# Outputs of 32 experts: stored by row of the token with an indirect DMA, instead of by slot and gathered afterwards

## What is computed

```python
u = rmsnorm(h, g_ffn)                         # 512 x 1024
g_idx = argmax(u @ w_group + b_group)         # one of 4 groups
top_v, top_i = top_k(within, 2)               # 2 of the 8 experts in that group
w_sel = softmax(top_v) * p_sel
for e in range(32):                           # D_EXPERT = 256
    hid = silu(u @ w1[e]) * (u @ w3[e])
    y = y + combine[:, e:e + 1] * (hid @ w2[e])
return h + y
```

## Time and profile before

| what | value |
|---|---|
| median of 3 runs | 713.04 us (712.62 to 713.07) |
| the profiled execution's own time | 711.57 us |
| its span | 710.1 us |
| busy PE / DVE / ACT / POOL | 84% / 33% / 29% / 19% of the span |
| share of 16 DMA engines, SP's queue | 45.1% (122.83 MB) |
| the same, ACT's queue (the stores of `yh`) | 3.3% (8.39 MB) |
| the same, POOL's software queue | 3.9% (8.53 MB) |

### The profile page before, as it was taken

One profiled execution on the slowest core, in us unless ns is written; L12 is line 12 of the kernel. 1 busy time (PEld: TensorE's weight loads), 2 busy tenths in 40 slices (PEclk: granted clock), 3 DMA queues, 4 the chain that ended last, 5 costly groups with the idle time before them and its releaser, 6 DMA issues.

```text
span 710.1 us, 9100 instructions
## 1 busy us (share of the span) xinstructions
PE 597.8 (84%) x3367; PEld 383.8 (54%) x3367; DVE 235.1 (33%) x511; ACT 207.2 (29%) x377; POOL 136.1 (19%) x208
## 2 busy tenths in 40 slices
PE   3699999999996988998999689987888788887830
PEld 3598688885663554664555345544444444444510
DVE  5652323233647483454255611111111111111105
ACT  6542314334553533553243311211111111111110
POOL 8200002111247521533100021111111111111022
PEclk9999999999999998999999889989999989999985
DMA  8900000019200010000400569999999999999938
GB/s 249 384 9 1 1 0 1 1 54 329 116 1 0 1 59 1 1 0 13 196 30 30 208 240 377 389 396 398 401 404 397 397 400 397 402 395 397 394 118 308
DMA packets 39056, 140.18 MB, mean 197 GB/s; under 512 B 8480, under 2 KB 10576, under 8 KB 30576
## 3 DMA queue, kind: packets, MB, share of 16 engines
q1 hardware_dynamic: 29680, 122.83, 45.1%
q0 software_dynamic: 4224, 8.53, 3.9%
q10 hardware_dynamic: 5120, 8.39, 3.3%
HBM read 131.28 MB, written 12.65 MB: 203 GB/s over the span
## 4 chain that ended last, share of the span: by engine, by line
PE 61%; DMA 15%; SPq 9%; DVE 7%; issue 4%; ACT 1%; POOL 1%; ACTq 0%; POOLq 0%; DVEq 0%
PE ps L1644 16%; DMA w<-in_w 11%; PE ps L1919 10%; PE ps L1683 7%; PE ps L1774 6%; PE ps L1763 6%; SPq L589 4%; PE ps L1946 3%; SPq L596 3%; PE ps L1827 3%; SPq L590 2%; PE ps L1739 2%; PE ps L1879 1%; DMA yg<-y_rows,pos_y 1%; DMA x<-in_x 1%
## 5 line engine op out<-in xcount | busy, mean ns | idle before, releaser
L1919 PE MATMUL ps<-w,xt 128*64 128x256 f32 x1024 | 134.8, 422 | 42.4 <-issue 32.0
L1919 PEld LDWEIGHTS ps<-w,xt 128*64 128x64 f32 x1024 | 88.3, 152 | 100.0 <-issue 74.9
L1509 DVE TENSOR_TENSOR xt<-ps,g_ffn_c 128x512 f32<-128x512 f32 x32 | 22.1, 691 | 231.3 <-PE ps L1879 231.3
L784 POOL DMA_INDIRECT xg<-u_rows,idx x32 | 29.8, 931 | 284.4 <-PE ps L1879 214.4
L1946 PE MATMUL ps<-w,hT 128*64 128x512 f32 x256 | 61.8, 604 | 0.0
L1068 ACT ACTIVATE hsb<-ps 128x256 f32<-128x256 f32 x32 | 12.3, 383 | 166.0 <-PE ps L1919 166.0
L1683 PE MATMUL ps<-w_oa,mixT 128*128 128x512 f32 x96 | 46.0, 616 | 2.0 <-issue 2.0
L1774 PE MATMUL ps<-probT,vals 128*128 128x512 f32 (+4 forms) x160 | 42.6, 410 | 0.0
L1763 PE MATMUL ps<-qT,kT 68*128 68x400 f32 (+9 forms) x160 | 42.2, 407 | 0.1
L1393 DVE TENSOR_REDUCE nmax<-ps 128x1 f32<-128x528 f32 (+1 forms) x64 | 28.0, 499 | 33.5 <-PE ps L1740 33.5
L719 POOL TENSOR_SCALAR_AFFINE_SELECT probT<-probT 128x128 f32<-128x128 f32 (+2 forms) x80 | 20.2, 271 | 87.7 <-ACT probT L991 87.2
(11 more groups left out here) (277 smaller groups left out, 899.4 us busy)
## 6 DMA issues: line engine op xcount, KB each, us to landing
w<-in_w SPq DMA_DIRECT2D x96, 1024.0 KB, 25.8
y_rows<-yh ACTq DMA_DIRECT2D x64, 128.0 KB, 6.7
w_oa<-in_w_o SPq DMA_DIRECT2D x1, 3072.0 KB, 17.5
x<-in_x SPq DMA_DIRECT2D x4, 512.0 KB, 7.3
w_in_v<-in_w_in SPq DMA_DIRECT2D x1, 2048.0 KB, 11.0
w_in_k<-in_w_in SPq DMA_DIRECT2D x1, 2048.0 KB, 16.0
w_in_q<-in_w_in SPq DMA_DIRECT2D x1, 2048.0 KB, 19.9
u_rows<-u2n SPq DMA_DIRECT2D x4, 512.0 KB, 2.6
```

The lines of the kernel that those rows point to most:

```text
L784: pool.indirect_dma_start(out=xg[e % 2][:, :, :].rearrange("p k n -> p (k n)"), out_offset=None, in_=u2_rows, in_offset=bass.IndirectOffse ...
L1919: ins = pe.matmul(ps[j * slots:(j + 1) * slots, 2 + b, 0:F], xt[b][:, k, :], w13[s][:, j, k, :], start=(k == 0), stop=(k == DK - 1))
```

## The change

The outputs of an expert are scattered at once to their tokens' rows. `y_rows` becomes 512 * 2 rows of 1024: row 2 * token + k for the token's choice k. Seen as half rows of 512 (`y_halves`), the half q of that row is number 4 * token + 2 * k + q, which fits the layout of `yh`.

- `pair_i` (2 * token + k, by POOL's iota) takes the place of `tok`; `pair_f` is 2 * pair - 2048 and is what `tok_hot` is multiplied by. `slot_hot` is 128 wide (the 64 slots twice) and made by two instructions. The index product so gives 128 rows. DVE adds `half_f` (2048 on the first 64 partitions, 2049 on the others) for `idy`, the half-row numbers, and shifts `idy` right by two for `idx`, the tokens. Empty slots are out of bounds in both.
- ACT no longer issues DMAs in the experts' loop. POOL issues one indirect DMA an expert (`scatter_rows`), four experts behind the gather that it follows in POOL's stream. It skips empty slots.
- The eight gathers at the end are gone. SP waits for all scatters and loads four tiles of 1 MB, in which each partition reads the two rows of its token, 8 KB in one piece, into `yg[t]`.
- The overflow branch is written anew to fit (not shown; it isn't taken), and `pos_y`, `late` and the zeroing of `y_over` are gone. The table's initial value is 1024 instead of 0.

```diff
-        yg = [place(f"yg{n}", [P, D], F32, r_qk + 4096 * n) for n in range(2 * NT)]
+        yg = [place(f"yg{t}", [P, 2, D], F32, r_qk + 8192 * t) for t in range(NT)]
...
+        slot_hot = late_new("slot_hot", [P, NT, 2, 2 * slots])
...
-        y_rows = nc.dram_tensor("y_rows", [MAIN + NE * REST, D], F32).ap()
+        y_rows = nc.dram_tensor("y_rows", [SEQ * 2, D], F32).ap()
...
+        y_halves = y_rows.rearrange("r (q d) -> (r q) d", q=2)
+        y_tiles = y_rows.rearrange("(t p k) d -> t p k d", p=P, k=2)
...
+            for b in range(2):
+                sp.wait_ge(y_stored[b], 16 * NE // 2)
+            for t in range(NT):
+                sp.dma_start(yg[t][:, :, :], y_tiles[t]).then_inc(yg_in[t], 16)
...
-            pool.iota(tok[:, :], pattern=[[P, NT]], base=0, channel_multiplier=1).then_inc(masks_made, 1)
+            pool.iota(pair_i[:, :, :], pattern=[[2 * P, NT], [1, 2]], base=0, channel_multiplier=2).then_inc(masks_made, 1)
...
-            step(pool.iota(tok_off[:, :], pattern=[[P, NT]], base=-SEQ, channel_multiplier=1))
-            pool.tensor_copy(tok_f[:, :], tok_off[:, :]).then_inc(masks_made, 1)
+            step(pool.tensor_copy(pair_f[:, :, :], pair_i[:, :, :]))
+            pool.tensor_scalar(pair_f[:, :, :], pair_f[:, :, :], 2.0, float(-2 * 2 * SEQ), ALU.mult, ALU.add
+                               ).then_inc(masks_made, 1)
...
-            step(pool.memset(zero_i[:, :], 0))
+            step(pool.memset(zero_i[:, :], 2 * SEQ))
...
+            def scatter_rows(e):
+                pool.wait_ge(y_copied, e + 1)
+                pool.indirect_dma_start(
+                    out=y_halves, out_offset=bass.IndirectOffsetOnAxis(ap=idy[:, e:e + 1].bitcast(U32), axis=0),
+                    in_=yh[e % 2][:, :], in_offset=None, bounds_check=2 * 2 * SEQ - 1, oob_is_err=False
+                ).then_inc(y_stored[e % 2], 16)
+
+            LAG = 4
             for e in range(NE):
...
+                if e == LAG:
+                    pool.wait_ge(idy_made, 1)
+                if e >= LAG:
+                    scatter_rows(e - LAG)
+            for e in range(NE - LAG, NE):
+                scatter_rows(e)
...
-            def fetch_outputs(source):
-                for b in range(2):
-                    pool.wait_ge(y_stored[b], 32 * NE // 2)
-                for t in range(NT):
-                    for k in range(2):
-                        n = 2 * t + k
-                        pool.indirect_dma_start(
-                            out=yg[n][:, :], out_offset=None, in_=source,
-                            in_offset=bass.IndirectOffsetOnAxis(ap=pos_y[:, t, k:k + 1].bitcast(U32), axis=0)
-                        ).then_inc(yg_in[n], 16)
...
-                    act.wait_ge(y_stored[b], 32 * (RING // 2 * it + s // 2))
+                    act.wait_ge(y_stored[b], 16 * (RING // 2 * it + s // 2))
                 act.activation(yh[b][:, :], ps[:, 6 + b, :], ACT.Copy).then_inc(y_copied, 1)
-                act.wait_ge(y_copied, e + 1)
-                for q in range(2):
-                    act.dma_start(y_main[e, :, q * 512:(q + 1) * 512], yh[b][q * slots:(q + 1) * slots, :]
-                                  ).then_inc(y_stored[b], 16)
...
+            step(dve.memset(half_f[:, :], float(2 * 2 * SEQ)))
+            dve.memset(half_f[slots:2 * slots, :], float(2 * 2 * SEQ + 1))
...
-                dve.tensor_scalar(tok_hot[:, i, :, :], ehots[:, i, :, :], tok_f[:, i:i + 1], None, ALU.mult)
+                dve.tensor_tensor(tok_hot[:, i, :, :], ehots[:, i, :, :],
+                                  pair_f[:, i, :].unsqueeze(2).to_broadcast([P, 2, NE]), ALU.mult)
...
-                dve.tensor_tensor(slot_hot[:, i, :, :], iota_f[:, :].unsqueeze(1).to_broadcast([P, 2, slots]),
-                                  ranks_all[:, i, :].unsqueeze(2).to_broadcast([P, 2, slots]), ALU.is_equal
-                                  ).then_inc(hot_made, 1)
+                for k in range(2):
+                    ins = dve.tensor_scalar(slot_hot[:, i, k, :].rearrange("p (q s) -> p q s", q=2),
+                                            iota_f[:, :].unsqueeze(1).to_broadcast([P, 2, slots]),
+                                            ranks_all[:, i, k:k + 1], None, ALU.is_equal)
+                ins.then_inc(hot_made, 1)
...
-            dve.tensor_scalar(idx[:, :], ps[0:slots, INDEX, 0:NE], float(SEQ), None, ALU.add).then_inc(idx_made, 1)
+            dve.tensor_scalar(idy[:, :], ps[:, INDEX, 0:NE], half_f[:, 0:1], None, ALU.add).then_inc(idy_made, 1)
+            dve.wait_ge(idy_made, 1)
+            dve.tensor_scalar(idx[:, :], idy[0:slots, :], 2, None, ALU.logical_shift_right).then_inc(idx_made, 1)
...
             for t in range(NT):
+                dve.wait_ge(yg_in[t], 16)
                 for k in range(2):
-                    n = 2 * t + k
-                    dve.wait_ge(yg_in[n], 16)
...
-                    ins = dve.scalar_tensor_tensor(out=x[:, t, :], in0=yg[n][:, :],
+                    ins = dve.scalar_tensor_tensor(out=x[:, t, :], in0=yg[t][:, k, :],
...
-                    ins = pe.matmul(ps[0:slots, INDEX, 0:NE], slot_hot[:, i, k, :], tok_hot[:, i, k, :],
+                    ins = pe.matmul(ps[:, INDEX, 0:NE], slot_hot[:, i, k, :], tok_hot[:, i, k, :],
```

## The result

The changed kernel takes 702.68 us (median of 4 runs, 702.35 to 705.39) against 713.06 (4 runs, 712.62 to 714.45): a ratio of 0.986, 95% interval 0.9831 to 0.9888, or 10.4 us less. I had forecast 14 less (699.0). The profiled execution has a span of 703.8 us, its own time is 705.39.

The account below looks back on a forecast made before the run. The experts were taken as bound by bytes through the 16 DMA engines. Experts 9 plus tail 5 gave 14 us off the 713.04 median, 699.0 us; the 8-in-10 range was 694.5 to 706.

Parts of the forecast that it names:

- the forecast's own range: Whole kernel: 695 to 702 us, from experts gaining 8 to 10.4 and the tail 4 to 7; chance 0.64.
- rival A: Tail: its loads are no faster than the gathers, so only the experts gain; 703 us, chance 0.12.
- The experts, forecast 9: Experts, 445 to 675 us: scatters of real rows replace full stores, freeing DMA engine time; 9 us gained.
- the uneven case: Experts' scatters: real rows fall unevenly on the 16 DMA engines; held mild, as some 30 rows per half load all nearly alike.
- My own bound: Experts' scatters, worst case: eight engines carry what sixteen do, 9.2% against 8.3% on the fullest, a loss of 2 us.
- The issue on POOL: Experts' loop: DMA issue moves from ACT to POOL, 0.93 to 0.97 us each, next gather keeps 3.9 us; costs nothing.
- Routing, forecast nothing: Before the first gather: index ready at 407.8 instead of 407.02, covered by 2.1 us of the token rows' store; uncovered 0.75 us.
- The tail, forecast 5: After the last product: earlier copy, one scatter and four 1 MB loads replace eight gathers; 23.3 us instead of 28.3.
- The bound of 7 us above: Tail, upper bound: all four loads stream at once from 686.5 with 2 us to the first byte; 7 us gained.
- B: Experts: empty slots still cost a packet or rows pile up on half the engines, only the tail gains; 708 us, chance 0.13.
- C: Experts: a 2 KB row written by index costs engines several times a direct one, so slower; 723 us, chance 0.06.
- D: Experts: the scatter blocks POOL over 3.9 us longer or lands after 16 us; 726 us, chance 0.03.

Follow-up runs that it names:

- the second profile: The changed kernel timed and profiled once more without edit: 702.77 us, ratio 0.9859.
- the slots spread: Changed kernel with each expert's tokens placed by another iota pattern over the 64 slots instead of in rank order: 699.07 us, then 699.26.
- the crowded run: Changed kernel with the opposite slot placement, each expert's first eight tokens in slots 0 to 3 and 32 to 35: 727.32 us, ratio 1.0206.

## Why the prediction was right, and where it was off

The sign and the range held: 702.68 lies in 694.5 to 706, but 0.7 above the forecast's own range of 695 to 702. The gain is 10.4 us instead of 14. The wider range reaches there because it takes in rival A, whose time was 703 by a mechanism that did not occur (a tail that gains 1 us); in that the range was lucky.

**The experts, forecast 9, measured 5.4 (5.1 in the second profile).** The sum was right for what it counted. The scatters' engine time was put at 4.6% of 230 us, 10.6 us, and is 9.7; freed is 9.4 us; the bytes' price by index is about that of the direct store. The step that failed is the next one: "I take 9", with unevenness left to the low end of the range. A queue's share is a mean over 16 engines and says nothing of the last of them to finish. This was mis-sized by about 4 us. With the slots spread, the stretch is 262.5 to 263.1, 9.6 to 10.1 us below before, and the forecast's 9 is there. The sentence that the uneven case is mild, drawn from the rule that some 30 rows in each half load all engines alike, took the average count for the counts: with 14 to 58 tokens, an expert leaves some groups empty or doubles others, and in rank order the extra ones are always at the low partitions. My own bound named the mechanism and a loss of 2 us against before, but for a case that I held unlikely; the crowded run is far past it, 17.6 us longer than before.

**The issue on POOL, forecast nothing: right.** 1.02 us an issue instead of 0.93 to 0.97, next wait for TensorE 3.0 us (forecast 3.9).

**Routing, forecast nothing: right, by 0.2 us.** The index is later by about 0.9 us relative to the last store of token rows (411.81 - 405.89 = 5.9 against 5.0); I had 0.75. The cover was misread: I took the 2.1 us up to the gather's start, but 0.95 of them are POOL's own start after its release, so 1.15 were there, and 0.17 and 0.26 us are left in two profiles.

**The tail, forecast 5, measured 4.7 and 5.1: right,** with its steps: counted from the last product, SP's first issue at 4.1 us (forecast 4.7), the last tile at 18.0 (17.7), the last add at 20.6 (20.3), the end at 23.7 (23.3). Two errors offset each other in this. The scatter lands 2.55 us after its start, where I took 4.0 from the first gather, and starts 0.8 us after the copy, where I had it start at once. The rule by which the receipt from HBM makes a small write slow (the Trainium skill, DMA: Bandwidth & Descriptors, Where the ~2 µs actually goes) would have meant more than that gather; this scatter took less. The four loads take 13.9 us from first issue to last landing instead of 13.0. The bound of 7 us above does not follow from its own terms: 686.5 + 2 + 10.5 us of bytes, two adds and the output store come to 704.7, a gain of 5.4.

**The rivals.** A is out: the tail gained all it should. B, the tail alone, is out as a case, though its second mechanism, rows that pile up, is what took 4 of the 9 us. C would have needed a scattered MB at 2 to 4 times the direct price; all slots scattered cost about what direct stores cost. D is out: with two scatters an expert POOL still waits for TensorE.

**What stays open.** What a second set of uneven scatters costs, and why the crowded placement costs more than the estimate. Why the gathers' unevenness costs so little in the kernel before. And which engines are the full ones: only the placement was varied.

## What to carry to other kernels

When a stage is bound by DMA engines, a transfer that skips rows saves its bytes' share of the time only if the rows that remain are spread over the engines; ask which partitions stay filled, and permute the slots (one iota here, worth 3.5 us and the fastest version, 699 us). A queue's share is a mean over 16 engines, and so is a forecast made from it: keep the worst engine as a case of its own. When a step is hidden behind a wait, count what is hidden to the release and not to the start of what waited. At the end of a kernel a few large direct loads of a layout that an earlier scatter has made beat several indirect gathers, since these come one issue at a time.

## What I had not expected of the hardware

- The busy share of the DMA engines stays at 1.01 to 1.02 while they work unevenly. The rate shows it only when it is gross (375 GB/s when crowded; 394 in both the changed and the spread kernel). The way the transfers run out at the end shows it in both cases (0.96 and 0.36 in successive 10 us against 0.99 and 0.23).
- A store by index of 2 KB pieces costs the engines about the same as a direct one: 2.7 against 2.8 us of the engines' time a MB, gathers included.
- POOL starts an indirect DMA some 0.95 us after its release: 0.93 to 0.95 us in nine of the ten profiles whose first gather the stored rows released.
- The time before the first gather varied between 409.1 and 414.3 us from one execution to another.
